# Scores of the attentions and of the stick as products over one head's 64 rows, without zero-padded copies of the queries

## What is computed

```python
# dilated branch, three groups, 8 heads of 64
s = jnp.einsum('nbqhd,nbkhd->nbhqk', qb, kb).astype(jnp.float32) * scale
s = jnp.where(valid[None, :, None], s + bias, -jnp.inf)
...
# stick-breaking attention of the second block, 8 heads of 64
z = jnp.einsum('bhqd,bhkd->bhqk', q[:, :, t0:t1], k[:, :, :t1]).astype(jnp.float32) * scale
causal = jnp.arange(t1)[None, :] < jnp.arange(t0, t1)[:, None]
log_1m = jnp.where(causal, jax.nn.log_sigmoid(-z), 0.0)
log_after = lax.cumsum(log_1m, axis=3, reverse=True) - log_1m
w = jnp.where(causal, jnp.exp(jax.nn.log_sigmoid(z) + log_after), 0.0)
```

## Time and profile before

| what | value |
|---|---|
| median of three runs | 3068.12 us (3066.44 to 3071.8) |
| profiled execution | 3062.41 us, span 3061.1 us |
| TensorE products | busy 2708.2 us, 88% of the span |
| TensorE weight loads | busy 2142.3 us, 70% |
| VectorE | 1222.5 us, 40% |
| ScalarE | 845.7 us, 28% |
| GpSimd | 511.7 us, 17% |

### The profile page before, as it was taken

One profiled execution on the slowest core, in us unless ns is written; L12 is line 12 of the kernel. 1 busy time (PEld: TensorE's weight loads), 2 busy tenths in 40 slices (PEclk: granted clock), 3 DMA queues, 4 the chain that ended last, 5 costly groups with the idle time before them and its releaser, 6 DMA issues. The chain is left out here.

```text
span 3061.1 us, 34956 instructions
## 1 busy us (share of the span) xinstructions
PE 2708.2 (88%) x13844; PEld 2142.3 (70%) x13844; DVE 1222.5 (40%) x2216; ACT 845.7 (28%) x1672; POOL 511.7 (17%) x595
## 2 busy tenths in 40 slices
PE   6999968689869999399899899997898899799997
PEld 5898958476555555286667687875697796587886
DVE  5533152242231111400553666525574563433333
ACT  2323231342121111110463321223422322332222
POOL 4564714300012222120000100001020110100001
PEclk9999978799979999699999899998998899899999
DMA  6332400002338999420001466522102102232322
GB/s 216 124 108 86 137 16 27 11 28 85 87 138 325 402 418 373 172 69 28 1 1 56 139 184 197 167 69 77 35 1 56 28 1 56 83 90 79 108 81 71
DMA packets 325649, 338.84 MB, mean 111 GB/s; under 512 B 19120, under 2 KB 296752, under 8 KB 313072
## 3 DMA queue, kind: packets, MB, share of 16 engines
q1 hardware_dynamic: 303280, 279.69, 27.8%
q0 software_dynamic: 22208, 56.93, 5.2%
HBM read 370.11 MB, written 16.78 MB: 126 GB/s over the span
## 5 line engine op out<-in xcount | busy, mean ns | idle before, releaser
L331 DVE TENSOR_TENSOR sb_w_lo<-sb_weights,sb_w_hi 128x1024 fp32r<-128x1024 f32 (+2 forms) x215 | 239.9, 1125 | 503.4 <-ACT sb_w_hi L325 503.2
L373 PE MATMUL bank<-sb_h_hi,sb_w_hi 128*128 128x512 f32 x1040 | 421.0, 405 | 11.6 <-DVE sb_w_lo L331 11.6
L375 PE MATMUL bank<-sb_h_hi,sb_w_lo 128*128 128x512 f32 x1040 | 408.4, 393 | 0.0
L374 PE MATMUL bank<-sb_h_lo,sb_w_hi 128*128 128x512 f32 x1040 | 407.9, 392 | 0.0
L325 ACT CAST sb_w_hi<-sb_weights 128x1024 fp32r<-128x1024 f32 x224 | 215.5, 970 | 554.4 <-PE bank L375 489.1
L414 POOL TENSOR_TENSOR sb_scratch<-sb_scratch 128x512 f32<-128x512 f32 x30 | 38.7, 1288 | 1320.5 <-ACT sb_scratch L404 1320.5
L913 PE MATMUL bank<-sb_weights,sb_hT 128*128 128x256 f32 x960 | 233.7, 400 | 14.2 <-DVE sb_padded L1361 12.3
L373 PEld LDWEIGHTS bank<-sb_h_hi,sb_w_hi 128*128 128x128 f32 x1040 | 196.8, 189 | 65.7 <-issue 25.7
L913 PEld LDWEIGHTS bank<-sb_weights,sb_hT 128*128 128x128 f32 x960 | 214.1, 286 | 23.6 <-issue 13.1
L374 PEld LDWEIGHTS bank<-sb_h_lo,sb_w_hi 128*128 128x128 f32 x1040 | 197.0, 189 | 45.6 <-issue 5.3
L375 PEld LDWEIGHTS bank<-sb_h_hi,sb_w_lo 128*128 128x128 f32 x1040 | 196.6, 189 | 43.2
(11 more groups left out here) (488 smaller groups left out, 4947.1 us busy)
## 6 DMA issues: line engine op xcount, KB each, us to landing
sb_weights<-ffn_w_in SPq DMA_DIRECT2D x88, 512.0 KB
sb_mod_weights<-ada_w POOLq DMA_DIRECT2D x24, 1024.0 KB, 5.6
sb_weights<-ada_w SPq DMA_DIRECT2D x24, 1024.0 KB
sb_expert_weights<-w_down SPq DMA_DIRECT2D x17, 1024.0 KB
sb_weights<-w_in SPq DMA_DIRECT2D x16, 1024.0 KB
sb_weights<-ffn_w_out SPq DMA_DIRECT2D x32, 512.0 KB
sb_weights<-gdn_w_in SPq DMA_DIRECT2D x32, 512.0 KB
sb_expert_weights<-w_up SPq DMA_DIRECT2D x14, 1024.0 KB
```

The lines of the kernel that those rows point to most:

```text
L331: dve.tensor_tensor(u.lo[:, 0:u.kt, :], u.chunk.w, u.hi[:, 0:u.kt, :].bitcast(F32), ALU.subtract).then_inc(*k.lo.one())
L373: pe.matmul(bank[:], u.hi[:, kk, :], act[0][:, kk, :], start=first and kk == 0, stop=False)
L374: pe.matmul(bank[:], u.hi[:, kk, :], act[1][:, kk, :], start=False, stop=False)
L375: mm = pe.matmul(bank[:], u.lo[:, kk, :], act[0][:, kk, :], start=False, stop=last and kk == u.kt - 1)
```

## The change

The scores take the queries and keys of one head directly, 64 partitions of each (`head_rows`), in the dilated groups, the causal attention of the second block, and at L2331 and L2341 of the stick. The padding copies, the padded tiles, their memsets, the two waits in `attention_pe` and `pad_queries` with its meet are removed.

```diff
@@ -305,6 +303,11 @@
     return slice(i * P, (i + 1) * P) if g == 0 else slice(i, S, STRIDE)
+def head_rows(h):
+
+    return slice(h % 2 * HD, (h % 2 + 1) * HD)
+
+
 def heads_of(view, heads):
     return view.rearrange("p (h d) -> p h d", h=heads)
...
@@ -558,9 +561,6 @@
             bank = k.bank[s % 3]
             if s >= 3:
                 pe.wait_ge(*k.exped.at(s - 2))
-            if padded and j.h == 0:
-                pe.wait_ge(*k.padded_even.at(j.tile + 1))
-                pe.wait_ge(*k.padded_odd.at(j.tile + 1))
             mm = pe.matmul(bank[:, 0:j.n], j.query, j.keys, start=True, stop=not j.bias)
             for i, (left, right, c) in enumerate(j.bias):
                 mm = pe.matmul(bank[:, c:c + right.shape[-1]], left, right, start=False, stop=i == len(j.bias) - 1)
@@ -597,29 +597,9 @@
             mm.then_inc(*k.finished.one())
-def pad_act(k, padded, i):
-    q, slots = padded
+def attention_act(k, jobs, normalise, out=None):
     act = k.nc.scalar
-    if i >= 2:
-        act.wait_ge(*k.scored.at(8 * (i - 1)))
-    act.copy(slots[i % 2][0:HD, 0:H:2, :], q[0:HD, :, i * P:(i + 1) * P]).then_inc(*k.padded_even.one())
-
-
-def pad_dve(k, padded, i):
-    q, slots = padded
-    dve = k.nc.vector
-    if i >= 2:
-        dve.wait_ge(*k.scored.at(8 * (i - 1)))
-    dve.tensor_copy(slots[i % 2][HD:P, 1:H:2, :], q[HD:P, :, i * P:(i + 1) * P]).then_inc(*k.padded_odd.one())
-
-
-def attention_act(k, jobs, padded, normalise, out=None):
-    act = k.nc.scalar
-    if padded:
-        pad_act(k, padded, 0)
     for s in range(len(jobs) + 7):
-        if padded and s % 8 == 4 and s // 8 + 1 < NT:
-            pad_act(k, padded, s // 8 + 1)
         if s < len(jobs):
             j = jobs[s]
             act.wait_ge(*k.maxed.at(s + 1))
@@ -642,13 +622,9 @@
                      ).then_inc(*k.mixed_in.one())
-def attention_dve(k, jobs, padded, normalise, out=None):
+def attention_dve(k, jobs, normalise, out=None):
     dve = k.nc.vector
-    if padded:
-        pad_dve(k, padded, 0)
     for s in range(len(jobs) + 7):
-        if padded and s % 8 == 4 and s // 8 + 1 < NT:
-            pad_dve(k, padded, s // 8 + 1)
         if s < len(jobs):
             j = jobs[s]
             dve.wait_ge(*k.scored.at(s + 1))
@@ -995,13 +971,14 @@
             lo = i - 1 if g == 0 and i > 0 else i
             for h in range(DIL_H):
                 dist = k.const(f"dist{g}")
-                jobs.append(Job(i, h, k.padded[i % 2][:, h, :], kt[:, h // 2, lo * P:(i + 1) * P],
+                jobs.append(Job(i, h, q[head_rows(h), h // 2, i * P:(i + 1) * P],
+                                kt[head_rows(h), h // 2, lo * P:(i + 1) * P],
                                 [], 1.0, [v[:, b, h * HD:(h + 1) * HD] for b in range(lo, i + 1)],
                                 k.negmax[:, g, i, h:h + 1], k.dens[:, g, i, h:h + 1],
                                 (dist[:, (1 - i + lo) * P:] if g == 0 else dist, 2.0 ** -(h + 1))))
-        attention_pe(k, jobs, True, False)
-        attention_act(k, jobs, (q, k.padded), False)
-        attention_dve(k, jobs, (q, k.padded), False, outs[g])
+        attention_pe(k, jobs, False)
+        attention_act(k, jobs, False)
+        attention_dve(k, jobs, False, outs[g])
         k.meet()
     modulation_end_dve(k, 0)
     combine(k, outs)
...
@@ -1355,11 +1332,7 @@
     k.open_area()
     k.arena = k.sb("arena", [P, 24 * S])
-    k.padded = [k.sb(f"padded{i}", [P, H, P]) for i in range(2)]
     k.more_weights(more)
-    for tile in k.padded:
-        k.nc.vector.memset(tile[:], 0.0).then_inc(*k.dve_step.one())
-    k.meet()
 def close_scores(k):
@@ -2311,16 +2284,7 @@
-def pad_queries(k, q, padded):
-    nc = k.nc
-    nc.gpsimd.memset(padded[0:HD, 1:H:2, :], 0.0).then_inc(*k.pool_step.one())
-    nc.vector.memset(padded[HD:P, 0:H:2, :], 0.0).then_inc(*k.dve_step.one())
-    nc.scalar.copy(padded[0:HD, 0:H:2, :], q[0:HD, :, :]).then_inc(*k.padded_even.one())
-    nc.vector.tensor_copy(padded[HD:P, 1:H:2, :], q[HD:P, :, :]).then_inc(*k.padded_odd.one())
-    k.meet()
-
-
-def stick_pe(k, padded, kb, vb, o):
+def stick_pe(k, qb, kb, vb, o):
     pe = k.nc.tensor
     for s in range(H + 2):
         h = s
@@ -2328,7 +2292,7 @@
             for j in range(NT):
                 if h >= 1:
                     pe.wait_ge(*k.reduced.at(4 * (h - 1) + j + 1))
-                pe.matmul(k.bank[j][:, 0:S - j * P], kb[:, h // 2, j * P:(j + 1) * P], padded[:, h, j * P:S],
+                pe.matmul(k.bank[j][:, 0:S - j * P], kb[head_rows(h), h // 2, j * P:(j + 1) * P], qb[head_rows(h), h // 2, j * P:S],
                           start=True, stop=True).then_inc(*k.scored.one())
         h = s - 1
         if 0 <= h < H:
@@ -2338,7 +2302,8 @@
                 pe.wait_ge(*k.reduced.at(4 * h + NT))
                 if m >= 3:
                     pe.wait_ge(*k.act_copied.at(m - 2))
-                pe.matmul(bank[:, 0:n], kb[:, h // 2, i * P:(i + 1) * P], padded[:, h, i * P:S], start=True, stop=False)
+                pe.matmul(bank[:, 0:n], kb[head_rows(h), h // 2, i * P:(i + 1) * P],
+                          qb[head_rows(h), h // 2, i * P:S], start=True, stop=False)
                 pe.matmul(bank[:, 0:P], k.const("ident"), k.const("sb_mask"), start=False, stop=False)
                 for j in range(i, NT):
                     mm = pe.matmul(bank[:, (j - i) * P:n], k.const("neg_from" if j == i else "neg_ones"),
@@ -2420,18 +2385,16 @@
     qa, ka, va, qb, kb, vb = (k.arena[:, j * 4 * S:(j + 1) * 4 * S].rearrange("p (a t) -> p a t", a=4)
                               for j in range(6))
     groups_project(k, qa, ka, va, qb, kb, vb)
-    jobs = [Job(i, h, k.padded[i % 2][:, h, :], ka[:, h // 2, 0:(i + 1) * P],
+    jobs = [Job(i, h, qa[head_rows(h), h // 2, i * P:(i + 1) * P], ka[head_rows(h), h // 2, 0:(i + 1) * P],
                 [(k.const("ident"), k.const("causal"), i * P)], HD ** -0.5,
                 [va[:, b, h * HD:(h + 1) * HD] for b in range(i + 1)], k.negmax_t[:, i, h:h + 1], k.den[:, i, h:h + 1])
             for i in range(NT) for h in range(H)]
-    attention_pe(k, jobs, True, True)
-    attention_act(k, jobs, (qa, k.padded), True, k.mixed[:, 0:4, :])
-    attention_dve(k, jobs, (qa, k.padded), True)
+    attention_pe(k, jobs, True)
+    attention_act(k, jobs, True, k.mixed[:, 0:4, :])
+    attention_dve(k, jobs, True)
     k.meet()
     o = qa
-    padded = k.arena[:, 4 * S:12 * S].rearrange("p (h t) -> p h t", h=H)
-    pad_queries(k, qb, padded)
-    stick_pe(k, padded, kb, vb, o)
+    stick_pe(k, qb, kb, vb, o)
     stick_act(k)
     stick_dve(k, o)
     k.meet()
```

More of the change, by code:

```diff
@@ L217, in __init__ @@
         self.mod_summed = Count(self, "DVE", "mod_summed")
-        self.padded_odd = Count(self, "DVE", "padded_odd")
         self.angled = Count(self, "DVE", "angled")
@@ L550, in __init__, with attention_pe @@
         self.n = keys.shape[-1]
-def attention_pe(k, jobs, padded, normalise):
+def attention_pe(k, jobs, normalise):
     pe = k.nc.tensor
```

4 lines of the change are left out of this document (removed).

## The result

The changed kernel takes 3198.97 us (median) beside 3067.28 us for the kernel before: ratio 1.0424, 95% interval 1.0401 to 1.0447. The forecast was +17 us; it is +132. The profiled execution has a span of 3197.1 us against 3061.1. The direction was right, the size wrong by a factor of nearly eight, and the time lies far outside the range.

What follows compares the result with a forecast made beforehand. TensorE was taken to bound group 0 and the causal attention, with waits in groups 1 and 2. Costs of 27.8 us less gains of 11.0 gave +16.8 on 3068.12, so 3084.9 us; range 3067 to 3100.

Steps and rivals of the forecast that it cites:

- the fourth rival: Loops and stick: nothing absorbed, 3109 us, or TensorE's clock drops longer because it idles between shapes; chance 0.08 beyond 3100.
- The passages: Changes between 128 and 64 rows around each score: 0.15 us in and 0.19 out, 0.34 us a score.
- the sum of 27.8 us: Costs together: group 0 +8.0, group 1 +2.6, group 2 +2.4, causal attention +10.3, stick +4.5 us.
- The stick: Passages around L2331 and L2341: +0.43 us a head for seven heads, +1.5 for the last, +4.5 in all.
- (a): Two memsets when the score area opens, twice, removed: 2.3 us each time, -4.6 us.
- (b): Padding copy at the start of each of four attentions removed: -0.7 us each, -2.8 us.
- (c): Padding ahead of the stick removed: -3.6 us.
- (d): Twelve padding copies within the loops removed: no gain, as TensorE will be the bound and covers them.
- (e): Two waits on TensorE at each tile removed: no gain, as the scores have their operands long before.
- No cost: First rival: 64-row scores cost nothing on entry and exit, only removals are left, 3053 us; chance 0.10.
- Side by side: Second rival: products over different halves of the rows run at once, halving the scores' share of TensorE, 3022 us; chance 0.02.
- Half hidden: Third rival: passages at half price in bound stages, none in groups 1 and 2, 11 against 11 us, 3068 us; chance 0.13.

Runs made afterwards that it cites:

- e8: Kernel before plus rows of bare products behind the three dilated groups, each row entered after TensorE stands for 3.3 to 3.4 us; 3495.22 us.
- e12: Kernel before plus bare products in the loops' mixes without waits, each mix once from a rest and once behind full products; 3575.94 us.
- e7: Kernel before with half-row stick, padded attentions, padded tiles cleared without an all-engine wait behind, first tile's padding copies during the projections; ratio 1.0003.
- e4: Kernel before plus rows of bare products behind the dilated groups, each led in by 24 full products of 512 columns at full clock; 3333.74 us.
- e6: Kernel before with a one-column product over 64 rows ahead of every second score of the padded attentions, scores still full-row; 3107.57 us, ratio 1.0136.
- e3: Kernel before with only the stick changed to 64-row products without padded queries, attentions still padded; 3067.48 us, ratio 1.0007.
- e11: e7 with a one-element exp on ScalarE ahead of each loop; ratio 0.9966 against the kernel before.
- e5: Kernel before with a one-column product over all 128 rows ahead of each score of the padded attentions; 3113.14 us, ratio 1.0154.

## Why the prediction was right or wrong

**The step that failed is the fourth rival's last sentence,** that the clock drops a level for longer because TensorE idles between shapes. The sum took every loop at the clock that it had, so the clock's term was nothing. In the rivals it had no price of its own and a chance of 0.08 with everything else beyond 3100, on the ground that these stages have 0.91 to 1.00 now. That number is the mean of one of two courses of a loop. It says that full-row jobs come back after a rest (in group 0 before: 0.50 in 130 to 134 us, 0.88 in 134 to 136), not that other jobs will. The jobs of the change don't come back, as e8 and e12 show without the loop around them and group 1 of e7 against that of the change within it. The rival's reason, that TensorE idles between shapes, was wrong as well: it is busy for 94 to 99% of the slow loops, and e4's blocks with a passage at every product keep 1.00. What makes the clock fall in the first jobs is only in part shown: TensorE rests there while the first exponentials are made, but the kernel before rests too and keeps its clock in group 1 and in the causal attention, and group 2 of e6 fell without such a rest. Priced as four loops of twice their length, the rival would have been 33.3 + 24.7 + 25.1 + 46.4 = 130 us. That this meets the measured +129.4 is partly chance: of group 0's added 1.42 us a score the passages are some 0.3 (2.52 less twice 1.10) and the clock the 1.10 that a doubled pace adds, and in groups 1 and 2 the passages take the place of waits that are gone. The Trainium skill, page "TensorE: Matmul & The Clock Gate", section "Part 1: The HAM clock gate (the "warmup" mystery)", says that activity of TensorE releases its throttle. By a reading of that as busy time the loops would have had the full clock; the rows have 94 to 99% busy at 0.52, and the measurement decides.

**The passages** were sized right for full clock: 0.34 us a score predicted, 0.34 in e12, 0.20 each in e4. In the loops, at the lower clock, it is 0.3 to 0.38. At full clock the sum of 27.8 us would have had its basis; that total itself is not shown, as no run kept the change's loops at full clock.

**Group by group.** Group 0 +33.4 for +8.0, group 1 +19.4 for +2.6, group 2 +19.0 for +2.4, causal +57.6 for +10.3. That group 1's scores would come evenly and without a pause at a tile's end was right in form (1.45 us apart, not 0.90).

**The stick** was +6.8 for +4.5, with 9.3 us more at the lower clock; by itself, in e3, it was +3.8. A steady head takes 13.41 us (1682.67 to 1696.08) against 13.08, +0.33 for the +0.43 predicted. Its wait ahead of the fourth L2305 (L2341 before) is still there, at 0.63, where I had put under 0.2: records of the first L2305 and of the next head's L2295, which use different halves, overlap (1684.29 and 1684.50), and that gave time back (timeline of TensorE, first and last scores of a head):

```profile
1682.67 1.98 PE L2295 MATMUL bank<-sb_arena 64*128 64x512 f32 x5
...
1692.87 0.46 PE L2305 MATMUL bank<-sb_arena 64*128 64x128 f32 x2 [0.63 <-ACT sb_scratch L2348]
```

**Removals.** (a) was right: TensorE starts its first projection at 30.11 in place of 32.79, -2.7 for the -2.3 predicted. (b), -0.7 at each of four loops, was wrong in sign: from TensorE's last product ahead of the loop to the first transpose it was +0.3, +0.6, +0.7 and +0.8, since the copy had also held the place of the table load. e7 and e11 show it: with the load put ahead again, e11 is shorter than before there by 0.95, 0.65, 0.65 and 0.72, which is the gain predicted. I had read only who ends last before the first score, and not what ScalarE did next. (c), -3.6 ahead of the stick, is -3.7 in e3; in the change only -1.0, as the causal loop's tail still runs in part at the lower clock. (d) and (e) can't be read beside the change of clock.

**The rivals.** "No cost" fell. "Side by side" was right as a mechanism: the first three scores of group 1 take 0.68 us against 0.91, and e4 shows it at its full size; against passages and clock it didn't count. "Half hidden" fell with the clock: nothing waits in these loops any more.

## What to carry to other kernels

Before you put a product of another shape into a loop, look not only at the clock that the loop has, but at where it rests and whether the new mix would bring the clock back from 1.2 GHz; where the clock before is 1.00, price the case that it stays at half, and expect twice the loop. If products over half the rows are wanted, issue two of different halves together, with nothing over full rows between them: that gave back four fifths of the loss here, though the narrow loops still ran at the lower clock. A small instruction ahead of a wait may hide a table load: when you remove it, see what now stands behind the wait.

## What the runs showed of the hardware that was not expected

- TensorE's clock has two lasting courses for the same work. Products over 64 rows, full and half rows in turn, and full products with one column between them keep 1.00 when they find it and nothing waits (blocks of 17 to 63 us, e4 and e12) and stay at 0.50 after a rest, for as long as the blocks lasted (51 to 120 us, e8 and e12); full rows alone and two halves side by side come back.
- A change between 64 and 128 rows costs 0.20 us at full clock, with 128 columns and with 512 (e4), and 0.30 at the lower one (e8, 256 columns); one between 96 and 128 rows costs nothing (0.22 us a product of 128 columns, as for full rows).
- Products over the low and the high 64 rows run fully side by side: 0.44 us each for 512 columns in place of 0.85.
- Two loops with the same jobs, groups 1 and 2 of e5, took 26.5 and 44.0 us.
